# Copying per-head preparation products out of PSUM with one VectorE copy, in a hybrid attention and mixture-of-experts layer

## What is computed

```python
def mla_q(p, g_qa, w_qb, g_q, cos, sin):
    cq = p[..., :MLA_Q_RANK]
    q = (rms_norm(cq, g_qa) @ w_qb).reshape(B, T, MLA_HEADS, MLA_QK_DIM)
    q = rms_norm(q, g_q)
    q = rope_tail(q, cos, sin)                 # rotates the last 64 of 192 columns

def mla_kv(p, g_kva, w_kvb, g_k, cos, sin):
    kv = (rms_norm(ckv, g_kva) @ w_kvb).reshape(B, T, MLA_HEADS, MLA_NOPE + MLA_V)
    k_nope, v = kv[..., :MLA_NOPE], kv[..., MLA_NOPE:]
    k = rms_norm(jnp.concatenate([k_nope, k_pe], axis=-1), g_k)
    k = rope_tail(k, cos, sin)                 # latent tokens only

def dense_attn_with_ctx(q, k, v, k_ctx, v_ctx, scale):
    s = einsum(qi, k_all) * scale
    p = softmax(s)
    return einsum(p, v_all)
```

## Time and profile before

| | us |
|---|---|
| median of three runs | 2024.27 |
| profiled execution, its own time | 2023.09 |
| its span, first to last instruction | 2021.3 |
| around the span | 1.8 |
| DVE busy | 834.7 (41%) |
| ACT busy | 434.3 (21%) |
| POOL busy | 179.6 (9%) |
| attention stage | about 554 to 880 |

### The profile page before, as it was taken

The page is one execution under the profiler, slowest core; times in us unless marked ns, Lnnn a source line. Parts: engine busy times, 40 slices in busy tenths (PEclk is TensorE's granted clock), DMA queues, the critical chain, the costliest instruction groups (busy, mean ns, idle before and its releaser), DMA issues.

```text
span 2021.3 us, 25844 instructions
## 1 busy us (share of the span) xinstructions
PE 1921.0 (95%) x10196; PEld 1218.5 (60%) x10196; DVE 834.7 (41%) x1711; ACT 434.3 (21%) x1141; POOL 179.6 (9%) x404
## 2 busy tenths in 40 slices
PE   4999999999999999999999999999989899998988
PEld 2588777888878888888877343535344353534423
DVE  5658878772256655544444140302213030221303
ACT  4332222222156555533222000000000000000000
POOL 0004112101133222200000000000000000000000
PEclk9999999999999999999999999999999999999999
DMA  9957888783032111242258999999999999999998
GB/s 403 421 199 290 317 291 308 283 296 140 27 112 82 46 46 46 88 178 105 104 215 362 427 390 428 428 427 427 427 428 427 428 427 428 427 428 428 428 426 352
DMA packets 79096, 603.32 MB, mean 298 GB/s; under 512 B 7792, under 2 KB 25456, under 8 KB 36224
## 3 DMA queue, kind: packets, MB, share of 16 engines
q1 hardware_dynamic: 65376, 590.06, 72.1%
q10 hardware_dynamic: 13168, 10.04, 1.5%
q0 software_dynamic: 432, 1.57, 0.2%
HBM read 584.85 MB, written 16.79 MB: 298 GB/s over the span
## 4 chain that ended last, share of the span: by engine, by line
PE 58%; DMA 9%; DVE 2%; ACT 2%; issue 1%; POOL 0%; DVEq 0%; ACTq 0%; POOLq 0%
DMA arena<-in_w_gate_up 9%; PE SM L1228 8%; PE TM L1228 8%; PE SM L1258 6%; PE TM L1258 6%; PE TR L1175 2%; PE TM L980 2%; PE MJ L1175 2%; PE SM L946 2%; PE MJ L871 1%; PE MJ L875 1%; PE SM L951 1%; PE SN L1215 1%; PE TM L971 1%; PE TM L1006 1%
## 5 line engine op out<-in xcount | busy, mean ns | idle before, releaser
L1228 PE MATMUL SM<-arena 128*64 128x512 f32 x1024 | 245.3, 599 | 39.7 <-DMA arena<-in_w_gate_up 39.7
L1228 PE MATMUL TM<-arena 128*64 128x512 f32 x1024 | 242.5, 592 | 0.0
L1825 DVE SCALAR_TENSOR_TENSOR arena<-arena,csil 128x512 f32<-128x512 f32 x240 | 180.4, 752 | 48.2 <-DMA arena<-in_w_mod 39.3
L1228 PEld LDWEIGHTS SM<-arena 128*64 128x64 f32 x1024 | 70.1, 136 | 178.4 <-issue 176.7
L1228 PEld LDWEIGHTS TM<-arena 128*64 128x64 f32 x1024 | 78.0, 137 | 141.8 <-issue 141.8
L1258 PE MATMUL SM<-arena 128*64 128x512 f32 x512 | 118.0, 610 | 0.8 <-DVE arena L2189 0.8
L1258 PE MATMUL TM<-arena 128*64 128x512 f32 x512 | 116.9, 598 | 0.0
L2097 DVE TENSOR_TENSOR brow<-cst,rope_t 128x512 f32<-128x512 f32 x8 | 5.5, 692 | 227.2 <-PE MJ L1201 227.1
L1542 ACT CAST y_hi<-arena 128x512 fp32r<-128x512 f32 x32 | 19.8, 618 | 370.1 <-DVE arena L2141 370.1
L1319 ACT ACTIVATE wh<-wr 128x2048 fp32r<-128x2048 f32 (+1 forms) x32 | 58.7, 1834 | 188.7 <-PE TN L775 133.9
L773 PE MATMUL SM<-wh,h_hi 128*128 128x512 f32 (+1 forms) x224 | 88.4, 395 | 6.5 <-DVE h_lo L1760 6.5
(11 more groups left out here) (360 smaller groups left out, 3472.4 us busy)
## 6 DMA issues: line engine op xcount, KB each, us to landing
arena<-in_w_gate_up SPq DMA_DIRECT2D x128, 2048.0 KB, 20.8
arena<-in_w_down SPq DMA_DIRECT2D x64, 2048.0 KB, 30.4
arena<-in_w_mod SPq DMA_DIRECT2D x96, 1024.0 KB, 5.3
wr<-in_w_na SPq DMA_DIRECT2D x24, 1024.0 KB, 7.0
wor<-in_w_out SPq DMA_DIRECT2D x8, 2048.0 KB, 7.9
xT<-in_tokens_t SPq DMA_DIRECT2D x4, 1536.0 KB, 12.5
arena<-in_w_qkv SPq DMA_DIRECT2D x8, 640.0 KB, 5.4
wr<-in_w_qa SPq DMA_DIRECT2D x4, 1024.0 KB, 17.9
```

What stands on the lines that cost most here:

```text
L1228: mm = pe.matmul(GU[b][64 * e:64 * e + CAP, :], xsT[:, k, 64 * e:64 * e + CAP], w[:, 2 * (b // 2) + e, (b % 2) * NB:(b % 2 + 1) * NB], sta ...
L1825: ve.scalar_tensor_tensor(acc, row, c, acc, ALU.mult, ALU.add).then_inc(mod_step, 1)
```

## The change

- take_prep on DVE now waits for the product itself (mj_full), no longer for ACT's square. It is a plain copy for queries (192 columns into m_nrm) and one copy of all 256 columns, keys and values together, for keys (into the new tile m_kv, of which m_v is now the second half). m_raw is gone.
- square_prep on ACT waits for that copy (mj_taken) and squares out of SBUF into an SBUF scratch, junk_m. ACT's own copy of V (L1403) is gone.
- Queries are no longer multiplied by gq_b. The gain of their first 128 columns goes, with MLA_SCALE, into gk_nope, once; that of the rotary columns goes into the tables cos2 and sin2 by three DVE multiplications (gain_tables), once, one slot before the first preparation product and after the keys' rotation, which needs the plain tables. POOL's first query rotation waits for them.
- The second place for preparation weights moves from 157.5 K to 193.5 K (the first from 109 K to 110.5 K), and load_qkv(1) is issued right after load_qkv(0).
- A column is added to the constants (gq_nope).

```diff
-        m_v = [arena.take(a + 10 * K, AT, VD) for a in m_at]
-        qkv_at = (109 * K, 157.5 * K)
+        m_kv = [arena.take(a + 8.5 * K, AT, NOPE + VD) for a in m_at]
+        m_v = [a[:, :, NOPE:NOPE + VD] for a in m_kv]
+        qkv_at = (110.5 * K, 193.5 * K)
...
-        m_raw = arena.take(104.5 * K, 2, NOPE)
+        junk_m = arena.take(198.5 * K, QK)
...
                     load_qkv(0)
+                    load_qkv(1)
...
             wait_used(sp, NW - 1)
-            load_qkv(1)
             load_bias(1)
...
             def square_prep(g, i):
 
                 m = PREP * g + i
-                sc.wait_ge(mj_full, m + 1)
+                sc.wait_ge(mj_taken, m + 1)
...
                 if i < LT:
                     c = 4 * (g % 2) + i
-                    sc.activation(M_JUNK, MJ[:, 0:QK], ACT.Square, accum_out=q_ss[:, c:c + 1]).then_inc(mj_squared, 1)
+                    sc.activation(junk_m, m_nrm[:, i % 3, 0:QK], ACT.Square, accum_out=q_ss[:, c:c + 1]).then_inc(mj_squared, 1)
                 else:
-                    sc.copy(m_v[g % 2][:, i - LT, :], MJ[:, NOPE:NOPE + VD])
-                    sc.activation(M_JUNK[:, 0:NOPE], MJ[:, 0:NOPE], ACT.Square,
+                    sc.activation(junk_m[:, 0:NOPE], m_kv[g % 2][:, i - LT, 0:NOPE], ACT.Square,
                                   accum_out=k_ss[:, i % 2:i % 2 + 1]).then_inc(mj_squared, 1)
...
-                        po.wait_ge(kpe_done, LT)
+                        po.wait_ge(gains_set, 6)
...
+            ve.scalar_tensor_tensor(gk_nope[:], gk_nope[:], MLA_SCALE, gq_nope[:], ALU.mult, ALU.mult).then_inc(gains_set, 1)
...
             def take_prep(g, i):
 
                 m = PREP * g + i
-                ve.wait_ge(mj_squared, m + 1)
+                ve.wait_ge(mj_full, m + 1)
                 if i < LT:
-                    ve.tensor_tensor(m_nrm[:, i % 3, 0:QK], MJ[:, 0:QK], gq_b[:], ALU.mult).then_inc(mj_taken, 1)
+                    if m >= 3:
+                        ve.wait_ge(mj_squared, m - 2)
+                    ve.tensor_copy(m_nrm[:, i % 3, 0:QK], MJ[:, 0:QK]).then_inc(mj_taken, 1)
                 else:
-                    if g or i >= LT + 2:
-                        ve.wait_ge(m_nrmd, AT * g + max(i - LT - 1, 0))
-                    ve.tensor_copy(m_raw[:, i % 2, :], MJ[:, 0:NOPE]).then_inc(mj_taken, 1)
+                    ve.tensor_copy(m_kv[g % 2][:, i - LT, :], MJ[:, 0:NOPE + VD]).then_inc(mj_taken, 1)
...
-                ve.tensor_scalar(m_nrm[:, i % 3, 0:NOPE], m_raw[:, i % 2, :], one, None, ALU.mult)
+                ve.tensor_scalar(m_nrm[:, i % 3, 0:NOPE], m_kv[g % 2][:, i - LT, 0:NOPE], one, None, ALU.mult)
...
+            def gain_tables():
+
+                ve.wait_ge(kpe_done, LT)
+                half = ROPE // 2
+                for table, gain in ((cos2, gq_b[:, NOPE:QK]), (sin2[:, :, 0:half], gq_b[:, NOPE + half:QK]),
+                                    (sin2[:, :, half:ROPE], gq_b[:, NOPE:NOPE + half])):
+                    ve.tensor_tensor(table, table, gain.unsqueeze(1).broadcast_to([P, LT, gain.shape[1]]), ALU.mult).then_inc(gains_set, 1)
...
+                if s == BLOCK_AT[5] - 1:
+                    gain_tables()
```

More of the change, by code:

```diff
@@ L415, in build_layer @@
         g1, g2, gqa, gkva, gq_b, gkt_b = (const(n) for n in ("g1", "g2", "gqa", "gkva", "gq_b", "gkt_b"))
-        gk_nope, gqn, gkn, gout = (const(n) for n in ("gk_nope", "gqn", "gkn", "gout"))
+        gk_nope, gq_nope, gqn, gkn, gout = (const(n) for n in ("gk_nope", "gq_nope", "gqn", "gkn", "gout"))
         bcol, bcol2 = const("bcol"), const("bcol2")
@@ L483, in build_layer @@
         LOGITS = [a[:, 256:256 + N_EXP] for a in AFF]
-        M_JUNK = MJ[:, 256:256 + QK]
         O = (TM[:, 768:768 + VD], TN[:, 0:VD])
@@ L1874, in turned_prep @@
                     ve.tensor_copy(m_k2T[a][half, at:at + P], TR[half, P:2 * P]).then_inc(tr_free, 1)
-            ve.wait_ge(gains_set, 2)
+            def gain_tables():
[4 more added lines that the diff above has]
+                    ve.tensor_tensor(table, table, gain.unsqueeze(1).broadcast_to([P, LT, gain.shape[1]]), ALU.mult).then_inc(gains_set, 1)
+            ve.wait_ge(gains_set, 3)
             for s in range(S_FROM, S_TO):
@@ L2219 @@
 CONST_SIZES = (("ident", P), ("cos2", LT * ROPE), ("sin2", LT * ROPE), ("sel", N_EXP), ("g1", KD), ("g2", KD), ("gqa", Q_RANK // P),
-               ("gkva", KV_RANK // P), ("gq_b", QK), ("gkt_b", ROPE), ("gk_nope", 1), ("gqn", 1), ("gkn", 1), ("gout", KD),
+               ("gkva", KV_RANK // P), ("gq_b", QK), ("gkt_b", ROPE), ("gk_nope", 1), ("gq_nope", 1), ("gqn", 1), ("gkn", 1), ("gout", KD),
                ("bcol", 2 * KD), ("bcol2", 2 * KD), ("slot_no", CAP), ("token_no", 2 * LT))
@@ L2289, in laid_out @@
         "gq_b": np.tile(g["g_q_mla"], (P, 1)), "gkt_b": np.tile(g["g_k_mla"][NOPE:], (P, 1)),
-        "gk_nope": columns(g["g_k_mla"][:NOPE]), "gqn": columns(g["g_q_na"]), "gkn": columns(g["g_k_na"]),
+        "gk_nope": columns(g["g_k_mla"][:NOPE]), "gq_nope": columns(g["g_q_mla"][:NOPE]), "gqn": columns(g["g_q_na"]), "gkn": columns(g["g_k_na"]),
         "gout": np.concatenate([columns(g["g_out_mla"]), columns(g["g_out_na"])], axis=1),
```

## The result

The changed kernel takes **2033.06 us** (median of five runs, 2032.28 to 2034.78), the kernel before beside it 2023.12 (2022.26 to 2027.12): ratio 1.0043, interval 1.0033 to 1.0054, so 9.9 us or 0.43% slower. The forecast was 2034.3 with a range of 2024 to 2041, and slower by more than 0.2% with a chance of 0.78. The profiled execution of the changed kernel took 2032.28 us, its span is 2030.5, against 2021.3 before.

The account below looks back on a forecast made before the run. PE was taken to bound the kernel, with attention delays absorbed nowhere. Five ordinary heads 8.3, head 2 1.23 and head 0 0.41 sum to +9.9 us; 2024.3 + 10.0 gives 2034.3 us, range 2024 to 2041.

Parts of the forecast that it names:

- What bounds the time: Whole kernel: PE works 95% of the span; a microsecond lost or won in attention moves everything behind it, nothing absorbs it.
- The chain and its four links: Each head: even units' B products, through ACT's square to late PE work; no slack left, 1.66 us added per ordinary head.
- (1) The order: Head of each chain: DVE copies before ACT squares, so the chain starts later, 0.39 us for queries, net 0.29 for keys.
- the delay is absorbed: Rival, attention: PE's transpositions or DVE's order set the exponential, so the later square hides; 2025 us, chance 0.13.
- (2) The SBUF square: ACT's square in each link: reading and writing SBUF instead of PSUM adds 0.01 us per link, 0.04 as upper bound.
- (3) The widths: Take ending the chain in units 3 and 5: 256 key columns for 128 add 0.13 us; queries add nothing.
- Head 2: The head that also splits w_out: 0.40 + 0.53 + 0 + 0.30 = 1.23 us slower.
- the zero for unit 5: Head 2: in unit 4 the earlier take starts L1950 about 0.2 us earlier, cancelling the longer copies; 0 for unit 5.
- it is worse: Rival, attention: POOL's delay of 0.4 us reaches PE's turns of query and key tiles; 2041 us, chance 0.15.
- (4) Head 0: Head 0: earlier load_qkv(1) and shorter handshake gain 0.85 us, units 3, 5, 7 pay 0.53, 0.43, 0.30; together +0.41.
- (5) What costs nothing: Gain-table and gk_nope products at about 475 us, head 0's rotation and roots: all covered; without cover at most 1.7 us.
- the bank's release decides: Rival, attention: B products wait for ACT's square, so removing it gives back the MJ waits; 2012.6 us, chance 0.10.

Follow-up runs that it names:

- The first experiment: Changed kernel with the B products of even units (27 of 70 products) again squared first, out of MJ, and copied after: 2024.55 us, ratio 0.9998.
- the exchange on DVE: In odd units, the take of product A moved ahead of the row maximum: 2018.61 us on the changed kernel, 2016.68 us on the kernel before.
- the third experiment: Kernel before with only DVE's take of a key product widened from 128 to 256 columns, ACT's copy of V kept: 2025.68 us, ratio 1.0012.

## Why the prediction was right, step by step

**What bounds the time.** Right. Nothing behind attention took up the loss: 9.4 us of lateness in attention, 9.2 between the spans, 9.9 between the medians.

**The chain and its four links.** Right, and the core of the case: the change made the wait that it addressed longer, since PE didn't wait for the square but for a take that was late in DVE's queue, and that queue was late through ACT. The first experiment took nearly all of the loss back with 27 products, and the exchange on DVE removed the stalls without touching the square.

**(1) The order.** Right in kind. The start of the square moved by 0.39 us as worked out. The links came to 0.31 for keys (0.30 predicted) but 0.30 for queries (0.40 predicted), so this term was mis-sized by 0.10 in units 1 and 3, about 1 us over the five heads. The reason stands in the earlier trace rows. There the copy L1453 starts 0.44 us after the square, though the same square needs only 0.32 when the next instruction is ready (in the kernel with the order alone). The copy takes out PE's transpositions L971, and these had ended just then:

```profile
736.44 0.60 PE L971 MATMUL TN<-cst,arena 128*128 128x128 f32 x4
```

In the changed kernel they end at 742.68, before the copy at 743.03. So 0.12 us of the later square was hidden, and the rival "the delay is absorbed" was true for three tenths of a query link. With it the sum comes out: 0.39 + 0.32 - 0.44 = 0.27 for the order alone (0.26 and 0.27 measured), 0.39 + 0.36 - 0.44 = 0.31 in the changed kernel (0.30 measured). I had noted that L1453 follows the square "at once" and didn't compare the distance of the two starts with what a square needs.

**(2) The SBUF square.** Mis-sized in the other direction: 0.04 per query link, not 0.01, the upper bound that I had kept. By line and shape, 600 to 845 us of the changed kernel:

```profile
L1403 ACT ACTIVATE arena<-arena 128x128 f32<-128x128 f32 x35 | 10.8, 309 | 32.6 <-DVE arena L1851 32.6
L1401 ACT ACTIVATE arena<-arena 128x192 f32<-128x192 f32 x24 | 8.7, 363 | 24.7 <-DVE arena L1849 24.7
```

The square of 192 columns took 0.32 us in the earlier trace rows and takes 0.363 here. The Trainium skill's 52 cycles, 0.043 us by my estimate ("VectorE: DVE Perf Modes", section on the TRN2 errata), describe the difference well (in its table the PSUM source goes with an SBUF output, here the earlier square wrote PSUM too); here the whole of it, and not a fraction, reached the query links.

**(3) The widths.** Right within 3 ns. Predicted 0.353 and 0.418 from the slope of the earlier trace rows:

```profile
L1851 DVE COPY arena<-MJ 128x256 f32<-128x256 f32 x35 | 14.7, 421 | 17.5 <-PE MJ L875 17.5
...
L1849 DVE COPY arena<-MJ 128x192 f32<-128x192 f32 x24 | 8.5, 355 | 25.0 <-PE MJ L871 25.0
```

The step of 0.13 at units 3 and 5 showed up alone in the third experiment.

**Head 2.** The step that failed is the zero for unit 5: +0.85 there, of which the collision is 0.72 to 0.78. The sum of the head is off by 0.2 only because other terms fell short: units 1 and 3 paid 0.46 together instead of 0.93, and unit 4 won 0.18. For units 1 and 3 the traces show a reason, which no run tested by itself. In unit 1 of the kernel before, the take of A starts 0.21 us after the last step of the row maximum instead of 0.13, since its square (L1401, 644.69) had come late behind ACT's split (L1481 at 643.74, 1.06 us); in the changed kernel it doesn't wait for the square and starts after 0.14. In unit 3 of the kernel before, mix_low follows DVE's split without idle time (655.42, the split from 654.29 on), so ACT doesn't set it; and PE waits 0.34 us there for the rotation of a query. In the changed kernel, where POOL's root of that query is held beside the split, this wait is 0.73:

```profile
656.79 1.22 DVE L1960 TENSOR_TENSOR wol<-wor,woh 128x1024 fp32r<-128x1024 f32 x1
...
656.94 1.48 POOL L1571 TENSOR_TENSOR st<-st,halves 128x1 f32<-128x1 f32 x1
...
659.80 0.30 PE L890 MATMUL TR<-cst,arena 128*128 128x128 f32 x1 [0.73 <-POOL arena L1587]
```

The B product follows at 660.05. With the rotation moved ahead, PE transposes at 659.19 without waiting and the product waits 0.70 us for the take instead: the two waits end at nearly the same time, and removing one gives nothing.

For unit 5 I had argued the cover from DVE's side only (the earlier take lets L1950 start earlier) and had not asked what the later square does to POOL's root beside L1950. The rival "it is worse" spoke of POOL, but of its delay of 0.4 eating up slack; for the rotations the run with the rotation moved ahead denies that, and the mechanism that did come was another, at one place instead of in every head.

**(4) Head 0.** The sum was near (+0.53 for +0.41), its parts not well divided. The rows of the changed kernel:

```profile
558.27 1.46 PE L871 MATMUL MJ<-arena 128*128 128x192 f32 x8
...
560.19 1.57 PE L871 MATMUL MJ<-arena 128*128 128x192 f32 x8 [0.45 <-DVE arena L1849]
...
566.28 0.69 DVE L1948 COPY arena<-TM 128x512 f32<-128x512 f32 x1 [4.06 <-DMA v_d<-arena]
567.12 1.58 PE L980 MATMUL TM<-arena 128*128 128x128 f32 x12 [0.85 <-DVE arena L1948]
```

The wait for in_w_qkv is gone and the next wait is 0.45 instead of 0.90, 1.8 us ahead at this point. Then DVE waits 4.06 us for the spill of V, which lands when it lands, and PE for DVE: 0.76 us are left at 567.12 and 0.66 from 568.73 on, where I had taken 0.85. In the other traces with the early load 0.44 to 0.89 us are left there. With the late load the loss is only 0.2 us greater: of what is left two thirds are due to the shorter handshake and not to the load. Units 3, 5 and 7 paid 0.43, 0.44 and 0.31.

**(5) What costs nothing.** True as far as the traces show: the four gain products leave no mark at 475 us, and the distance between the traces there is that of any two runs. In one place, unit 3 of head 2, PE does wait longer for POOL's rotation (above), at no cost. The rival in which the bank's release decides had its point only in head 0, in that one handshake.

**The total.** 9.9 predicted, 9.4 measured in the attention. It is so near in part because errors cancel: the query links were 1 us too dear, head 2 and head 0 together 0.3 too cheap.

What stays open: the 0.18 that unit 4 of head 2 won, the 0.14 and 0.26 that the widened take alone adds in its units 4 and 5 (the third experiment), and why executions differ by up to 4 us ahead of the attention.

## What to carry to other kernels

Before a handshake is shortened, look at whether the instruction that releases the waiting engine had idle time ahead of it. If it had none, its place in its own queue is what makes it late, and the cure is its place: moving the take of the A products ahead of a row maximum was worth 16 us in the changed kernel, and reversing the handshake lost 9. Where two engines read the same product, the one that heads the longer chain should read first, even if the other could free the buffer sooner.

To price a delay, compare the distance between the starts of the delayed instruction and of the next one with what the instruction needs by itself: what is over is slack that was hidden. And follow the delay onto each engine that waits for it, asking what wide instruction of another engine it will now fall under.

## What of the hardware was unexpected

- A one-column instruction of POOL that falls under DVE's split (two inputs in SBUF, 1024 columns, 1.21 us) lasts until that ends: 1.50 us for 0.27, in the changed kernel and in the kernel before with this one product taken first, though by its record it had started 0.16 us earlier. With the product squared first, this step is over before the split starts.
- A square of 192 columns takes 0.04 us longer out of SBUF than out of PSUM, and this whole difference shows in the start of the next instruction.
- Two executions of kernels that are the same in the first 540 us stand up to 4 us apart by then, so a single span can't tell a change of 2 us; the lateness of the same matmul from there on could tell 0.05.
